# Two-block transformer on one core: the first mixer's tokens are turned before their norm, the norm factor goes onto the drains

## The reference, cut to what matters

```
def rmsnorm(x, g):
    xf = x.astype(jnp.float32)
    y = xf * lax.rsqrt(jnp.mean(xf * xf, axis=-1, keepdims=True) + NORM_EPS)
    return (y * g.astype(jnp.float32)).astype(x.dtype)
...
z = rmsnorm(x, mix_norm_ab[i]) @ w_in_ab[i]
o_a = mla_mixer(z[..., :IN_A], ...)
o_b = dilated_mixer(z[..., IN_A:], slopes)
```

## Time and profile before

| | us |
|---|---|
| median of 3 runs (1867.55 to 1867.99) | 1867.93 |
| the profiled execution's own time | 1868.62 |
| its span in the trace | 1865.8 |
| TensorE busy (matmuls) | 1845.1 |
| VectorE busy | 1334.5 |
| ScalarE busy | 857.8 |

### The profile page before, as it was taken

The page is one execution under the profiler, slowest core; times in us unless marked ns, Lnnn a source line. Parts: engine busy times, 40 slices in busy tenths (PEclk is TensorE's granted clock), DMA queues, the critical chain, the costliest instruction groups (busy, mean ns, idle before and its releaser), DMA issues.

```text
span 1865.8 us, 27862 instructions
## 1 busy us (share of the span) xinstructions
PE 1845.1 (99%) x10520; PEld 1588.8 (85%) x10520; DVE 1334.5 (72%) x1677; ACT 857.8 (46%) x1081; POOL 138.5 (7%) x167
## 2 busy tenths in 40 slices
PE   9999999999999999999999999999999999999998
PEld 8988888888888888888878888888888887788887
DVE  5577767786767877776776776677767767677777
ACT  5554344564334533444475433344335347544433
POOL 1002100330000110000300100010000021000000
PEclk9999999999999999999999999999999999999999
DMA  7524555425555665544444465566555444445553
GB/s 293 181 91 164 188 202 181 168 92 214 192 195 188 236 233 197 186 164 170 168 149 167 173 213 186 196 228 224 200 180 174 165 169 147 158 181 214 183 200 112
DMA packets 48641, 341.59 MB, mean 183 GB/s; under 512 B 5568, under 2 KB 5600, under 8 KB 9136
## 3 DMA queue, kind: packets, MB, share of 16 engines
q1 hardware_dynamic: 42912, 308.82, 46.4%
q0 software_dynamic: 5648, 31.62, 4.4%
HBM read 338.32 MB, written 1.05 MB: 182 GB/s over the span
## 4 chain that ended last, share of the span: by engine, by line
PE 64%; DVE 1%; ACT 1%; issue 0%; POOL 0%; DVEq 0%; POOLq 0%
PE bank L1098 16%; PE bank L889 12%; PE bank L890 11%; PE bank L891 11%; PE bank L1100 8%; PE bank L952 1%; PE bank L1551 1%; PE bank L1177 1%; PE bank L997 1%; PE bank L992 1%; PE bank L993 1%; DVE wlo L2113 0%; DVE share L2830 0%; PE bank L1475 0%; PE bank L1413 0%
## 5 line engine op out<-in xcount | busy, mean ns | idle before, releaser
L2113 DVE TENSOR_TENSOR wlo<-raw,whi 128x2048 fp32r<-128x2048 f32 x290 | 667.1, 2303 | 214.1 <-ACT whi L1618 212.4
L1618 ACT ACTIVATE whi<-raw 128x2048 fp32r<-128x2048 f32 x291 | 555.3, 1909 | 247.1 <-PE bank L891 244.3
L1098 PE MATMUL bank<-ysp,whi 128*128 128x512 f32 x1920 | 480.2, 392 | 0.0
L1098 PEld LDWEIGHTS bank<-ysp,whi 128*128 128x128 f32 x1920 | 348.6, 189 | 64.6
L1100 PEld LDWEIGHTS bank<-ysp,wlo 128*128 128x128 f32 x1920 | 261.9, 190 | 18.7
L1100 PE MATMUL bank<-ysp,wlo 128*128 128x256 f32 x1920 | 267.7, 282 | 0.0
L1701 ACT ACTIVATE sg<-sg 128x256 f32<-128x256 f32 x120 | 50.1, 418 | 466.7 <-DVE sg L2318 466.7
L889 PE MATMUL bank<-whi,ysp 128*128 128x512 f32 (+3 forms) x592 | 217.4, 367 | 4.2 <-DVE wlo L2113 2.8
L891 PE MATMUL bank<-whi,ysp 128*128 128x512 f32 (+3 forms) x592 | 212.7, 359 | 0.0
L890 PE MATMUL bank<-wlo,ysp 128*128 128x512 f32 (+3 forms) x592 | 212.4, 359 | 0.0
L889 PE MATMUL bank<-whi,hl 128*128 128x512 f32 x528 | 206.5, 391 | 0.0
(11 more groups left out here) (364 smaller groups left out, 2196.9 us busy)
## 6 DMA issues: line engine op xcount, KB each, us to landing
raw<-stream SPq DMA_DIRECT2D x292, 1024.0 KB, 4.8
sr<-side POOLq DMA_DIRECT2D x10, 1024.0 KB, 6.9
gbc<-gains POOLq DMA_DIRECT2D x11, 512.0 KB, 3.9
cw<-small POOLq DMA_DIRECT2D x2, 2048.0 KB, 10.6
gbias<-gate_rows POOLq DMA_DIRECT2D x6, 512.0 KB, 3.7
lng<-rows POOLq DMA_DIRECT2D x2, 1024.0 KB, 5.1
tab<-second POOLq DMA_DIRECT2D x1, 1724.0 KB, 16.1
dbias<-dilb POOLq DMA_DIRECT2D x1, 1536.0 KB, 12.2
```

What stands on the lines that cost most here:

```text
L1098: pe.matmul(o, hi[:, k, cols], ysp[:, :, k, :], start=k == 0, stop=False, skip_group_check=True)
L1618: act.activation(whi[s], raw[s], ACT.Copy).then_inc(hi_made, 1)
L2113: dve.tensor_tensor(wlo[s], raw[s], whi[s].bitcast(F32), ALU.subtract).then_inc(lo_made, 1)
```

## The change

x is multiplied by the gains alone (`unscaled`) and turned at once; the norm factor of each token is applied when the steps are drained. In steps 0 to 2 and for the values the tokens are in the rows of the bank, so ScalarE drains each half with the factor as its scale. In steps 3 to 8 the tokens are in the columns: a row of factors, the same in every partition, is made by scaling the identity (`rdiag`) and multiplying it with ones (two fp32 matmuls between steps 2 and 3), copied twice into `rrow`, times 0.125 for the queries; VectorE drains these steps with a product (`rows_scaled`). The squares of the second half move behind the hi copy of tile 1, their mean behind its lo part. The identity comes by a transfer of its own that ScalarE issues, POOL loads the rest of `misc`. x's second half is issued ahead of tile 0. `opening_step` makes all hi x hi products of the first half, then turns the second half, then makes the others.

```diff
-PLAN1.weights("z", "A" * 11)
+PLAN1.weights("z", "AAADDDDDDAA")
...
+        rrow = at("rrow", A + 12 * K, 2 * S, shape=(2, S))
+        rdiag = at("rdiag", A + 14 * K, M * P, shape=(M, P))
...
             sp.dma_start(gbc, gains[0]).then_inc(gain0_in, 16)
+            sp.dma_start(x[:, 1, :], xin[:, 1, :]).then_inc(x_in[1], 16)
             sp.dma_start(raw[0], stream[0]).then_inc(landed[0], 16)
-            sp.dma_start(x[:, 1, :], xin[:, 1, :]).then_inc(x_in[1], 16)
...
-            pool.dma_start(misc_sb, misc).then_inc(tab_in, 16)
+            pool.dma_start(misc_sb[:, P:], misc[:, P:]).then_inc(tab_in, 16)
...
-            halves_power()
+            power(1, dst=rfirst)
+            power(1, dst=rfirst, at_=1)
...
-            for _ in range(18):
+            for _ in range(16):
                 pe.matmul(pb[4][:, 0:P], ones, ones, start=True, stop=True)
-            pe.wait_ge(tab_in, 16)
+            pe.wait_ge(ident_in, 16)
...
                 for m in range(M):
                     t = slice(m * P, m * P + P)
-                    if m:
+                    for k in range(8):
+                        if k % 4 == 0:
+                            copied_by(B, 2 * m + k // 4 + 1, "A")
+                        if m == 0 and k % 2 == 0:
+                            pe.wait_ge(first_hi, k // 2 + 1)
+                        pe.matmul(pb[0][:, 256 * m:256 * m + 256], yh[:, k, t], hi[:, k, :], start=k == 0, stop=False)
+                    if m == 0:
                         turn(B, "n0", 0, 1, 0)
                         turn(B, "n0", 0, 1, 1)
...
             for i in range(1, 9):
+                if i == 3:
+                    pe.wait_ge(rdiag_made, 1)
+                    for m in range(M):
+                        last = pe.matmul(pb[4][:, m * P:m * P + P], ones, rdiag[:, m, :], start=True, stop=True)
+                    last.then_inc(rrow_summed, 1)
                 dense(B, "z", i, "T" if i < 3 else "F", n=160 if i == 2 else 256)
...
-            needs = {g: lambda g=g: pe.wait_ge(drain_act, B.drained(B.plan.step["z"] + 7 + g, "A")) for g in range(DG)}
+            needs = {g: lambda g=g: pe.wait_ge(drain_dve, B.drained(B.plan.step["z"] + 7 + g, "D")) for g in range(DG)}
...
+            act.dma_start(ident, misc[:, 0:P]).then_inc(ident_in, 16)
             sumsq(0, parts=(0, 1))
...
-            sumsq(0, parts=(2, 3))
-            split(B, 1)
             hi_norm(B, "n0", 1, 0)
             hi_norm(B, "n0", 1, 1)
+            split(B, 1)
+            sumsq(0, parts=(2, 3))
+            act.wait_ge(rstd_ready, 2)
+            act.wait_ge(ident_in, 16)
+            for m in range(M):
+                ins = act.activation(rdiag[:, m, :], ident, ACT.Copy, scale=rfirst[:, m:m + 1])
+            ins.then_inc(rdiag_made, 1)
             for i in range(9):
                 ahead(B, "z", i)
-                stepped(B, "z", i)
                 if i < 3:
+                    stepped(B, "z", i)
                     n = 256 if i < 2 else 160
-                    ins = act.activation(zA[:, :, 256 * i:256 * i + n], bank2(i % 2)[:, :, 0:n], ACT.Copy)
-                else:
-
-                    ins = act.activation(dqk[:, 2 * i - 6:2 * i - 4, :], bank2(i % 2), ACT.Copy, scale=0.125 if i < 6 else 1.0)
-                ins.then_inc(drain_act, 1)
+                    for m in range(M):
+                        ins = act.activation(zA[:, m, 256 * i:256 * i + n], bank2(i % 2)[:, m, 0:n], ACT.Copy, scale=rfirst[:, m:m + 1])
+                    ins.then_inc(drain_act, 1)
+                if i == 2:
+                    act.wait_ge(rrow_summed, 1)
+                    for j in range(2):
+                        ins = act.activation(rrow[:, j, :], pb[4][:, 0:S], ACT.Copy, scale=(0.125, 1.0)[j])
+                    ins.then_inc(rrow_ready, 1)
...
-            norm(0, gain0_in, 16, gbc, (0,))
+            def unscaled(m, q):
+
+                c = slice(512 * q, 512 * q + 512)
+                dve.tensor_tensor(y[:, m, c], x[:, m, c], gbc[:, c], ALU.mult).then_inc(y_ready, 1)
+
+            dve.wait_ge(gain0_in, 16)
+            for m in range(M):
+                dve.wait_ge(x_in[m], 16)
+                for q in range(2):
+                    unscaled(m, q)
...
-            norm(0, gain0_in, 16, gbc, (1,))
+            half_mean(0, 0)
             lo_norm(B, "n0", 1, 0)
             lo_norm(B, "n0", 1, 1)
             split(B, 1)
+            half_mean(0, 1)
             for i in range(4):
                 ahead(B, "z", i)
...
+            def rows_scaled(i):
+
+                stepped(B, "z", i)
+                dve.tensor_tensor(dqk[:, 2 * i - 6:2 * i - 4, :], bank2(i % 2), rrow[:, i // 6, :].unsqueeze(1).broadcast_to([P, 2, S]),
+                                  ALU.mult).then_inc(drain_dve, 1)
+
+            dve.wait_ge(rrow_ready, 1)
             for i in range(4, 9):
+                rows_scaled(i - 1)
                 ahead(B, "z", i)
+            rows_scaled(8)
```

More of the change, by code:

```diff
@@ L378, in build @@
         rstd = little("rstd", 24)
+        rfirst = little("rfirst", 2)
         half = little("half", 24)
@@ L526, in build @@
         tab_in = sem("tab_in")
+        ident_in = sem("ident_in")
+        rdiag_made = sem("rdiag_made")
+        rrow_summed = sem("rrow_summed")
+        rrow_ready = sem("rrow_ready")
         mlag_in = sem("mlag_in")
@@ L1243, in opening_step @@
                     t = slice(m * P, m * P + P)
-                    if m:
+                    for k in range(8):
[5 more added lines that the diff above has]
+                    if m == 0:
                         turn(B, "n0", 0, 1, 0)
                         turn(B, "n0", 0, 1, 1)
[L1247 to L1259, removed]
+                    for k in range(8):
+                        if k % 4 == 0:
+                            copied_by(B, 2 * m + k // 4 + 1, "D")
+                        pe.matmul(pb[0][:, 256 * m:256 * m + 256], yl[:, k, t], hi[:, k, :], start=False, stop=False)
+                    for k in range(8):
+                        if m == 0 and k % 2 == 0:
+                            pe.wait_ge(first_lo, k // 2 + 1)
+                        last = pe.matmul(pb[0][:, 256 * m:256 * m + 256], yh[:, k, t], lo[:, k, :], start=False, stop=k == 7)
                 last.then_inc(step_done, 1)
@@ L1653, in sumsq @@
                     c = slice(512 * (j % 2), 512 * (j % 2) + 512)
-                    act.activation(y[:, j // 2, c], x[:, j // 2, c], ACT.Square, scale=D ** -0.5,
+                    act.activation((zsq if type(n) is int and n == 0 else y)[:, j // 2, c], x[:, j // 2, c], ACT.Square, scale=D ** -0.5,
                                    accum_out=ss[:, j // 2, j % 2:j % 2 + 1]).then_inc(ss_act, 1)
@@ L1810, in values @@
                 stepped(B, stage, i)
-                act.activation(dv[:, :, 256 * j:256 * j + 256], bank2(0), ACT.Copy).then_inc(drain_act, 1)
+                for m in range(M):
+                    ins = act.activation(dv[:, m, 256 * j:256 * j + 256], bank2(0)[:, m, :], ACT.Copy, scale=rfirst[:, m:m + 1])
+                ins.then_inc(drain_act, 1)
             def queries(i):
```

## The result

The changed kernel takes 1871.42 us (median of 20 runs, 1869.78 to 1872.40) against 1867.95 for the kernel before (20 runs, 1867.55 to 1869.09): ratio 1.0017, interval 1.0011 to 1.0023. It is 3.5 us slower where +0.8 was forecast, and lies above the range (1866.8 to 1871.0). The profiled execution took 1871.75 us, its span is 1869.6. Its runs spread over 2.6 us, those of the kernel before mostly over 0.5.

What follows compares the result with a forecast made beforehand. TensorE was taken to bound the kernel nearly everywhere (busy 1845.1 of 1865.8 us). The terms -1.2 + 0.1 + 0.5 + 1.3 + 0.1 gave +0.8, so 1868.7 us, range 1866.8 to 1871.0.

Steps and rivals of the forecast that it cites:

- Opening, -1.2: At the kernel's front: step 1 of the first projection begins at 19.65 in place of 20.82, a gain of 1.2 us.
- Tile 2, +0.1: Weight tile 2's split, behind ScalarE's factor work, is done at 25.15, asked for at 25.4; 0.1 us taken for slips.
- row of factors, +0.5: Two fp32 matmuls of 128 columns between steps 2 and 3 cost TensorE 0.5 us, uncovered.
- The stall, +1.3: Step 5 waits 1.3 us, to 44.2, for the bank of step 3, whose VectorE drain stands behind the MLA norm chain.
- I take 32.0: Landing time taken for weight tile 5, from 4.35 MB at 0.4 MB a us being in by 31.7; 35.0 kept for the range.
- rival 2: Tile 5 comes late, sharing DMA engines with the bias table; step 5 moves by 2.7 us at the bound: 1871.4 us; chance 0.12.
- The steady rate: DMA from 20.8 us on: 0.4 MB a us, for tiles 4 and 5 and POOL's three loads.
- The estimate by queues that take turns: DMA engines serve queues with work packet by packet; tile 5 gets half the rate from about 26.4, in by about 31.3.
- the row of 9.8 us: Profile row: three tiles loaded beside such traffic took 9.8 us in the median, which would put tile 5 at 35.0.
- Rival 3: TensorE's clock falls to 1.2 GHz ahead of the opening step: up to 5.76 us more, some 1874 us; chance 0.05.
- Smaller things, +0.1: Six drains in halves, of zA and the values, cost ScalarE some 0.15 us each; between 0 and 0.45, 0.1 taken.
- No further loss once past the stall: After step 3's late drain, VectorE has 2.3 + 0.7 us of work in a step of 5.76, so no more is lost.

Runs made afterwards that it cites:

- the opening alone: Changed kernel without the row of factors, its copies and waits; ScalarE drains steps 3 to 8 in one piece, dqk lacks the norm factor: 1867.12 us, before 1867.90.
- bias table moved: Changed kernel with POOL's 1.5 MB bias table load issued behind the power of the MLA norm, near 40 us instead of 20.6: 1869.12 us, before 1867.85.
- the drain ahead of the norm: Changed kernel, but VectorE drains step 3 before the norm of the MLA latents instead of behind it: 1868.47 us, before 1867.90.
- fewer waits: The drain ahead of the norm, without TensorE's repeated waits for VectorE drain counts it has already waited for: 1867.31 us, before 1867.85.
- eleven fillers: The kernel with fewer waits, with eleven filler matmuls instead of six ahead of the opening step: 1867.13 us, before 1867.85.
- fillers in the stall: Changed kernel with nine filler matmuls of the identity in TensorE's queue ahead of step 5: 1869.80 us, before 1867.90.
- values in one piece: The drain ahead of the norm, with the values drained by ScalarE in one piece and their norm factor left out: 1867.24 us.

## Why the prediction was wrong

- **Opening, -1.2.** Right, mechanism and size: -1.39 in the trace (19.43 for 20.82), -1.25 at the end of the span with the opening alone.
- **Tile 2, +0.1; row of factors, +0.5.** Right: tile 2's lo began at 22.61 and was no hindrance; the two matmuls took 0.4.
- **The stall, +1.3.** The mechanism was right, at the place and in the one wait that was named. The size was not: 2.4 us. Step 3 began 0.4 earlier than worked out and the drain ended 0.9 later. The step that failed is "I take 32.0" for tile 5. It was there at 33.1, inside the bounds I kept, so rival 2 was true in part, and with the bias table moved the stall is 1.2. The steady rate was right (396 GB/s); the sum had left out tile 6 in the same queue, and nothing said that the stream would move no byte for the first 3.4 us. The estimate by queues that take turns, 31.3, was 1.8 too early, and the row of 9.8 us said too much, it took 8.
- **The clock.** This is the step that failed most. Rival 3 had it at 0.05, in one place, and only for a wait of 1.5 us; I argued that 1.27 us of waiting did no harm in the kernel before. The forecast itself contained a stall in mid-stream and priced it at its own length. In fact the fall behind it costs 1.5 us more in this execution, and in the opening the clock falls in up to half of the executions, 1.2 us each, where rival 3 had 5.8. That term was missing from the sum, and it is larger than the 1.3 forecast for the stall. Without it the longer stall would have stayed inside the range: the two runs whose mean clock rules a fall out took 1869.78 and 1869.83.
- **Smaller things, +0.1.** 0.5 in the trace. The halves, for which the 0.1 stood, cost nothing where the repeated wait is absent; that repeated wait of TensorE, which the plan's count adds by itself, stood in no line of the diff and was not priced.
- **The sum**, as the profiled execution has it: -1.4 + 0.4 + 2.4 + 1.5 + 0.5 = 3.4 and 0.4 that I can't place; 3.8 in the span, 3.5 in the medians. For the runs without a fall it is -1.4 + 0.4 + 2.4 + 0.5 = 1.9, as measured. That the median of 1871.42 is the figure of rival 2 (1871.4) is luck: its late tile gave 1.1 of its 2.7 us, the clock most of the rest.
- **No further loss once past the stall** was right: the other five drains fit beside the tiles.

The kernel with the drain ahead of the norm, the fewer waits and eleven fillers keeps some of the gain: 1867.13 us against 1867.85, ratio 0.9997 with an interval of 0.9987 to 1.0006, so below what the comparison can tell, though ten of its eleven runs lie under all 33 runs of the kernel before.

## What to carry to other kernels

When a drain is moved to another engine, look where it stands in that engine's order, not how busy the engine is: one drain behind a chain of 7 us cost more than six drains' work. Price a stall of the engine that bounds the kernel at more than its length if the clock may fall behind it, and where a wait can't be avoided put work into it. And ask what a plan's counts do to waits elsewhere: a semaphore that was zero for a stage becomes one more wait in each of its products.

## What the runs showed that I had not expected

- The granted clock fell to 0.50 for about 3.3 us after 2.42 us of standing still (changed kernel) and after 1.42 us followed by a half-filled step (the drain ahead of the norm), and did not after 1.2 us (bias table later) or after 1.27 us in the kernel before. It is not the same in each execution: of four kernels with the same opening (the drain ahead of the norm, fillers in the stall, values in one piece, fewer waits) 5 or 6 runs in 11 are 1.1 to 1.3 us slower, and in the profiled executions of the changed kernel and of the one with fewer waits the same 1.4 us of waiting brought no fall.
- A wait for a semaphore that has long been reached costs TensorE 0.10 to 0.14 us at three of ten places, two of them beside a wait that does block, and nothing at seven.
- POOL's loads took the DMA engines for themselves for 3.4 us while the stream moved nothing, and ScalarE stood 1.1 us for weight tile 5. With the 1.5 MB table moved, the tiles issued from 16 to 40 us landed in 4.8 us in the median (8.0 before that).
